# Two token tiles through each stage transition of a two-block network: together, or one ahead of the other

## What is computed

```
x = [256, 1024]                                   # BATCH 1, SEQ 256
for i in range(2):                                # first block
    sh1, sc1, g1, sh2, sc2, g2 = split(silu(c) @ ada_w[i] + ada_b[i])
    h = rms_norm(x, norm_mix[i]) * (1 + sc1) + sh1
    y = chunked_relpos_attention(h) if i == 0 else chunked_spatial_gating(h)
    x = x + g1 * y
    h = rms_norm(x, norm_ffn[i]) * (1 + sc2) + sh2
    x = x + g2 * (square(relu(h @ ffn_w1[i])) @ ffn_w2[i])
for l in range(2):                                # second block
    h = rms_norm(x, pre_norm_g[l]);  proj = h @ w_in[l]      # q, k, v, gates of two attentions
    y = concat(ya, yb) @ w_out[l]
    x = x + rms_norm(y, post_norm_g[l])
```

## Time and profile before

| | us |
|---|---|
| median of 3 runs | 1133.7 (1127.31 to 1136.37) |
| the profiled execution's own time | 1133.17 |
| its span, first to last instruction | 1131.5 |
| PE busy | 1081.2 |
| DVE busy | 768.0 |
| ACT busy | 554.4 |
| mean granted TensorE clock | 0.947 of full |

### The profile page before, as it was taken

The page is one execution under the profiler, slowest core; times in us unless marked ns, Lnnn a source line. Parts: engine busy times, 40 slices in busy tenths (PEclk is TensorE's granted clock), DMA queues, the critical chain, the costliest instruction groups (busy, mean ns, idle before and its releaser), DMA issues.

```text
span 1131.5 us, 18346 instructions
## 1 busy us (share of the span) xinstructions
PE 1081.2 (96%) x6096; PEld 931.3 (82%) x6096; DVE 768.0 (68%) x1352; ACT 554.4 (49%) x933; POOL 92.4 (8%) x146
## 2 busy tenths in 40 slices
PE   6998979999999999999999999999999989899897
PEld 6877867899989878889998789998878768688685
DVE  5787667887887567777877555465487464675663
ACT  1556756434543356634443344354355563545552
POOL 1121101000000000100000000000011020120100
PEclk8799988799999889999999799999999999799989
DMA  9875555588778358865765265546266410466111
GB/s 373 314 256 193 196 187 186 171 295 292 268 268 298 135 179 280 302 216 201 254 220 189 88 212 201 177 164 216 67 211 221 137 56 20 158 206 202 57 33 51
DMA packets 58071, 219.12 MB, mean 194 GB/s; under 512 B 6532, under 2 KB 12420, under 8 KB 51880
## 3 DMA queue, kind: packets, MB, share of 16 engines
q1 hardware_dynamic: 49232, 170.02, 43.7%
q0 software_dynamic: 5760, 41.95, 10.4%
q10 hardware_dynamic: 3032, 6.57, 1.8%
HBM read 217.46 MB, written 1.06 MB: 193 GB/s over the span
## 4 chain that ended last, share of the span: by engine, by line
PE 78%; issue 8%; DVE 7%; DMA 2%; ACT 2%; POOL 2%; DVEq 0%; SPq 0%; ACTq 0%; POOLq 0%
PE ps L1593 23%; PE ps L1594 22%; PE ps L1595 22%; PE ps L1660 2%; PE ps L1688 2%; DVE w_lo L947 2%; PE ps L1678 1%; PE ps L1642 1%; POOL rinv L439 1%; DMA ada_raw<-in_adastream 1%; PE ps L1955 1%; PE ps L1652 1%; ACT ada_raw L630 1%; PE ps L2061 1%; DVE h_lo L1028 1%
## 5 line engine op out<-in xcount | busy, mean ns | idle before, releaser
L947 DVE TENSOR_TENSOR w_lo<-raw,w_hi 128x1024 fp32r<-128x1024 f32 (+1 forms) x318 | 359.3, 1172 | 58.9 <-ACT w_hi L533 53.2
L533 ACT ACTIVATE w_hi<-raw 128x1024 fp32r<-128x1024 f32 (+1 forms) x318 | 308.7, 1009 | 127.9 <-DMA raw<-in_wstream 90.7
L1593 PE MATMUL ps<-h_hi,w_hi 128*128 128x256 f32 x704 | 203.1, 288 | 0.7 <-DVE h_lo L1028 0.5
L1595 PE MATMUL ps<-h_hi,w_lo 128*128 128x256 f32 x704 | 201.4, 286 | 0.0
L1594 PE MATMUL ps<-h_lo,w_hi 128*128 128x256 f32 x704 | 201.4, 286 | 0.0
L1593 PE MATMUL ps<-w_hi,h_hi 128*128 128x512 f32 (+1 forms) x480 | 193.8, 404 | 3.2 <-DVE h_lo L1028 3.2
L1594 PE MATMUL ps<-w_lo,h_hi 128*128 128x512 f32 (+1 forms) x480 | 188.3, 392 | 0.0
L1595 PE MATMUL ps<-w_hi,h_lo 128*128 128x512 f32 (+1 forms) x480 | 188.2, 392 | 0.0
L1593 PEld LDWEIGHTS ps<-h_hi,w_hi 128*128 128x128 f32 x704 | 137.6, 195 | 3.7 <-issue 2.2
L1593 PE MATMUL ps<-w_hi,a_hi 128*128 128x512 f32 x352 | 137.4, 390 | 0.7 <-DVE a_lo L1356 0.7
L1594 PEld LDWEIGHTS ps<-h_lo,w_hi 128*128 128x128 f32 x704 | 137.4, 195 | 0.7
(11 more groups left out here) (186 smaller groups left out, 1347.7 us busy)
## 6 DMA issues: line engine op xcount, KB each, us to landing
raw<-in_wstream SPq DMA_DIRECT2D x296, 512.0 KB, 5.4
ada_raw<-in_adastream POOLq DMA_DIRECT2D x40, 1024.0 KB, 5.4
ada_raw<-in_adastream SPq DMA_DIRECT2D x4, 1024.0 KB, 9.0
arena<-in_adastream SPq DMA_DIRECT2D x4, 1024.0 KB, 10.6
raw<-in_wsmall SPq DMA_DIRECT2D x22, 128.0 KB, 2.2
row<-in_gate_rows ACTq DMA_DIRECT2D x5, 512.0 KB, 3.9
row<-in_params ACTq DMA_DIRECT2D x2, 769.0 KB, 4.0
x<-in_x SPq DMA_DIRECT2D x1, 1024.0 KB, 9.0
```

The costliest lines, as they stand in the source:

```text
L533: act.activation(w_hi[:, c % SPLIT, at], raw[:, n, 0:width // 2], ACT.Copy)\
L947: nc.vector.tensor_tensor(w_lo[:, c % SPLIT, at], raw[:, (2 * c + h) % RAW, 0:width // 2], w_hi[:, c % SPLIT, at].bitcast(F32), ALU.subtract)\
L1593: nc.tensor.matmul(dst, sh, mh, start=start, stop=False)
L1595: return nc.tensor.matmul(dst, sl, mh, start=False, stop=stop)
```

## The change

**Every transition runs tile by tile.** The last products of a stage are ordered so that tile 0's banks end first (`last_downs`: tile 0's products of both chunks, then tile 1's; the attention's and the second block's output steps likewise). The residual, the squares, the scaling, the transposes, the modulation and the operand's split are then written for one tile at a time, in halves of four k-blocks: 128-column ACT instructions in place of 256-column ones (twice as many), the same number of transposes and of DVE instructions. PE issues 4 matmuls of zeros before tile 0's transposes and 8 behind them. The first products of the next stage are made for tile 0, then tile 1 is transposed between them, then tile 1's products follow.

**In the FFNs** the first two `up` chunks are therefore made with the tokens stationary (`up_tile`, 96 matmuls of 256 columns, as many as before); their results are copied out by ACT, transposed back by PE (`turn_up`, 4 transposes for each chunk) and then go through relu and square.

**In the gating** the shift and scale columns (`columns(36, 4)`) move between tile 0's and tile 1's last products, and DVE's last two conditioning sums (`ada(46)`, `ada(47)`) move from before the transition to behind it. In the attention `columns(12, 5)` moves ahead of tile 1's last two output steps.

**In the second block** the four small chunks become one chunk of full width (`heads_tile`), `project_tile` runs over two chunks (CL+1, CL+2) with the second tile's transposes between them, the layers and the gating's groups are written out instead of looped, and the splits next to the transitions are placed anew: of chunk CL+2, `lo_part(CL + 2, 0)` comes behind tile 0's operand and `lo_part(CL + 2, 1)` behind tile 1's.

Shortened to what the text below speaks of (ACT's part first, then DVE's, then PE's):

```diff
+            def square(t, count):
+
+                act.wait_ge(s_res, count)
+                act.activation(both[:, t * D:(t + 1) * D], x[:, t, :], ACT.Square,
+                               accum_out=ss2[:, t:t + 1]).then_inc(s_sq, 1)
+
+            def modulate(t, count, scale, shift):
+
+                for half in range(2):
+                    act.wait_ge(s_xT, count + 2 * t + half + 1)
+                    for k in range(4 * half, 4 * half + 4):
+                        last = act.activation(f[:, k, t * P:(t + 1) * P],
+                                              ps[:, 4 + 2 * t + half, (k % 4) * P:(k % 4 + 1) * P],
+                                              ACT.Identity, scale=scale[:, k:k + 1],
+                                              bias=shift[:, k:k + 1] if shift is not None
+                                              else zero_col[:])
+                    last.then_inc(s_f, 1)
...
+
+                split(c0 + 3)
+                for u in range(2):
+                    act.wait_ge(s_used, c0 + u + 1)
+                    act.activation(squared[:, u, :], ps[:, 2 * u, :], ACT.Copy)\
+                        .then_inc(s_upraw, 1)
+                    act.wait_ge(s_upT, m0 // 14 + u + 1)
+                    act.activation(relu[:, u, :], ps[:, 4 + u, :], ACT.Relu).then_inc(s_upread, 1)
+                    act.wait_ge(s_upread, 2 + m0 + u + 1)
+                    act.activation(a_hi[:, u].rearrange("p a b -> p (a b)"), relu[:, u, :],
+                                   ACT.Square).then_inc(s_acthi, 1)
+                for j in range(1, 4):
+                    split(c0 + 3 + j)
...
+            split(C_WO + 5)
+            square(0, 1)
...
+            modulate(0, 4, mod_scale[:, 1], mod_shift[:, 1])
+            square(1, 2)
+            modulate(1, 4, mod_scale[:, 1], mod_shift[:, 1])
+            split(C_WO + 6)
...
-                squares(4, lambda t: act.wait_ge(s_res, layer * 2 + (6 + t + 1)))
-
...
+
+                act.wait_ge(s_pre, layer * 16 + 16)
+                modulate(0, layer * 4 + 16, prenorm, None)
...
-                    act.wait_ge(s_xT, layer * 4 + (16 + pr + 1))
-                    for b in range(2):
-                        k = 2 * pr + b
-                        last = act.activation(f[:, k, :], ps[:, 4 + pr, b * S:(b + 1) * S],
-                                              ACT.Identity, scale=prenorm[:, k:k + 1],
...
+
+                i = 2 * t + cb
+                dve.wait_ge(*ready[i])
+                cut = slice(cb * 512, (cb + 1) * 512)
+                own.inc(nc.vector.tensor_tensor(y_tmp[:, i, :], ps[:, cb * 2 + t, :], gate[:, cut],
+                                                ALU.mult))
+                own.wait()
+                last = nc.vector.tensor_tensor(x[:, t, cut], x[:, t, cut], y_tmp[:, i, :], ALU.add)
+                if cb == 1:
+                    last.then_inc(s_res, 1)
...
+            def transition(ready, count, at_first, before_second, behind):
+
+
+                residual(0, 0, ready)
+                residual(0, 1, ready)
+                at_first()
+                residual(1, 0, ready)
+                norm_x(0, count // 2)
+                residual(1, 1, ready)
+                operand(0, count)
+                before_second()
+                norm_x(1, count // 2)
+                operand(1, count)
+                behind()
...
+                modulation(1, 5)
+                lo_part(C_WO + 4, 1, CW)
...
-                    operand(8)
+                    transition(ready, 8, lambda: None, lambda: lo_part(c0 + 34, 0, CW),
+                               lambda: lo_part(c0 + 34, 1, CW))
                 else:
...
+            def gated_modulation():
+                modulation(3, 4)
+
+            transition([(s_bank, 4), (s_bank, 5), (s_bank, 6), (s_used, C_FFN[1])], 12,
+                       gated_modulation, lambda: None, lambda: split(C_FFN[1] + 2))
+            ada(46)
+            ada(47)
             mlp_stage(1, 28, False)
...
+                norm_x(0, layer * 2 + 8)
+                operand(0, layer * 4 + 16)
+                lo_part(CL + 2, 0, CW)
+                norm_x(1, layer * 2 + 8)
+                operand(1, layer * 4 + 16)
+                lo_part(CL + 2, 1, CW)
+                lsplit(3)
...
+                if layer + 1 < DEPTH:
+                    lsplit(C_LAYER)
...
+                if layer + 1 < DEPTH:
+                    lsplit(C_LAYER + 1)
...
+            def project_tile(c, bank, h_base, t, between=None):
+
+                for half in range(2):
+                    chunk_in(c + half)
+                    for n in range(4):
+                        k = half * 4 + n
+                        operand_in(h_base, t, k)
+                        last = matmul3(ps[:, bank, :], tokens(k, t), weights(c + half, 512, n),
+                                       k == 0, k == KT - 1)
                     if t == 1:
                         last.then_inc(s_used, 1)
-
...
+                for k in range(KT):
+                    last = nc.tensor.transpose(
+                        ps[:, 4 + 2 * t + k // 4, (k % 4) * P:(k % 4 + 1) * P],
+                        xn[:, t, k * P:(k + 1) * P], ident[:])
+                    if k % 4 == 3:
+                        last.then_inc(s_xT, 1)
+
+            def transition(count):
+                keep_warm(7, WARM[0])
+                transpose_x(0, count)
+                keep_warm(7, WARM[1])
...
+            def up_tile(c, u, t, ks, h_base):
+
+                for k in ks:
+                    operand_in(h_base, t, k)
+                    last = matmul3(ps[:, 2 * u, t * AW:(t + 1) * AW], tokens(k, t),
+                                   weights(c + u, AW, k), k == 0, k == KT - 1)
+                if t == 1 and ks[-1] == KT - 1:
+                    last.then_inc(s_used, 1)
+
+            def turn_up(u, count):
+
+                pe.wait_ge(s_upraw, count + u + 1)
+                for b in range(2):
+                    for t in range(TT):
+                        last = nc.tensor.transpose(
+                            ps[:, 4 + u, b * S + t * P:b * S + (t + 1) * P],
+                            squared[:, u, t * AW + b * P:t * AW + (b + 1) * P], ident[:])
+                last.then_inc(s_upT, 1)
...
+                for t in range(TT):
+                    for u in range(2):
+                        if t == 0:
+                            chunk_in(c + 2 + u)
+                            pe.wait_ge(s_act, m + u + 1)
+                        for cb in range(2):
+                            last = down_products(c, u, t, cb, u == 1)
+                            if u == 1 and (t, cb) != (1, 1):
+                                last.then_inc(s_bank, 1)
+                        if t == 1:
+                            last.then_inc(s_used, 1)
+                    if t == 0 and between is not None:
+                        between()
...
+                transition(2 * n)
+                chunk_in(c0)
+                up_tile(c0, 0, 0, range(KT), 4 * n + 4)
+                transpose_x(1, 2 * n)
+                chunk_in(c0 + 1)
+                up_tile(c0, 1, 0, range(KT), 4 * n + 4)
+                up_tile(c0, 0, 1, range(KT), 4 * n + 4)
+                up_tile(c0, 1, 1, range(4), 4 * n + 4)
+                turn_up(0, 2 * layer)
+                up_tile(c0, 1, 1, range(4, KT), 4 * n + 4)
+                for bank in (0, 1, 3):
+                    zero_bank(bank)
+                turn_up(1, 2 * layer)
+                zero_bank(2)
+                for u in range(2):
+                    down(c0, u, m0 + u, None, 4, lambda v: v)
+                with pe.Fori(0, 6) as i:
                     for u in range(2):
-                        up(c0, u, m0 + u, i, 4, lambda v: i * 2 + v, h_base)
...
+            transition(4)
+            pe.wait_ge(s_gelu, 2)
+            project_tile(C_GV, 0, 12, 0, lambda: transpose_x(1, 4))
+            project_tile(C_GV, 1, 12, 1)
...
+            def gated_columns():
+                pe.wait_ge(s_upread, 2 + 28)
+                pe.wait_ge(s_ada, 44)
+                columns(36, 4)
...
+                else:
+                    last_downs(c, m, gated_columns)
...
+                def heads_tile(t):
+                    chunk_in(CL)
+                    for k in range(KT):
+                        operand_in(layer * 8 + 20, t, k)
+                        last = matmul3(ps[:, t, 0:S], tokens(k, t), weights(CL, S, k), k == 0,
+                                       k == KT - 1)
+                    last.then_inc((s_half, s_used)[t], 1)
...
+                heads_tile(0)
+                project_tile(CL + 1, 2, layer * 8 + 20, 0,
+                             lambda: transpose_x(1, layer * 2 + 8))
+                heads_tile(1)
+                project_tile(CL + 1, 3, layer * 8 + 20, 1)
```

More of the change, by code:

```diff
@@ L486, in _ @@
             norm(3)
-            with pool.Fori(0, DEPTH) as layer, own.loop(layer, DEPTH, 15):
+            for layer in range(DEPTH):
```

(11 more changed lines are left out.)

558 lines of the change are left out of this document (258 added, 300 removed).

## The result

| | before | after |
|---|---|---|
| median, us (15 runs each) | 1133.35 (1127.31 to 1139.92) | 1142.53 (1138.1 to 1147.15) |
| profiled execution's own time, us | 1133.17 | 1139.18 |
| its span, us | 1131.5 | 1137.5 |
| mean granted clock | 0.947 | 0.953 |

The ratio is 1.0082, 95% interval 1.0058 to 1.0107: some 9.2 us slower by the medians, where 10.6 had been predicted.

The account below looks back on a forecast made before the run. PE's own time was taken as the bound (busy 96%), with losses in five transition gaps and half clock behind them. Terms -0.8 - 3.2 + 0.4 + 5.6 + 8.2 + 0.4 = +10.6 on 1133.17 gave 1143.8 us; range 1126 to 1153.

Parts of the forecast that it names:

- rival A: The forecast itself: second-tile waits and half clock as summed, 1134 to 1153 us; chance 0.6.
- second-tile waits: PE waiting inside stages for work queued behind tile 1's operand: 4.9 us in each second-block layer's `project_tile`.
- transition 2: FFN 0 to gating: first product at E+4.2 (E is the last product's end), gap and block -3.2 us.
- Transition 4: FFN 1 to layer 0: first product E+5.6, 4.9 us wait in `project_tile`, half clock 2.5; +5.6 us in all.
- transition 5: Layer 0 to layer 1: first product E+12.1 or E+13.3, the same 4.9 us wait and half clock; +8.2 us.
- Transition 1: Attention to FFN 0: first product at 199.8 (before 203.7), down products at 216.5 against 217.9; -0.8 us.
- the wait of 1.4 for the conditioning sum: Transition 1: PE reaches the moved columns at 183.6 and waits 1.4 us for DVE's sum, ending near 185.1.
- the 1.7 us before tile 1's transposes at transition 2: Transition 2: PE has made half of tile 0's products by E+7.0 and waits 1.7 us for tile 1's norm.
- Transition 3: Gating to FFN 1: earlier first product, but two conditioning sums delay the first activation, PE idle some 3.6 us; +0.4 us.
- B: Rival: the clock stays up behind the gaps; -2.8 us, 1130 us (1125 to 1136); chance 0.2.
- C: Rival: the second tile's work is never late, leaving gaps and transposes alone; -22 us, 1111 us (to 1122); chance 0.08.
- D: Rival: chunk CL+4 comes late, each second-block layer losing 5 us more; 1154 us (1148 to 1160); chance 0.12.

Follow-up runs that it names:

- experiment 1: Changed kernel with both halves of chunk CL+2 split ahead of tile 1's norm and modulation in both second-block layers; 1133.89 us, ratio 1.0022 to the kernel before.
- experiment 2: Changed kernel with the gating's last two conditioning sums moved back ahead of the transition to FFN 1; 1136.17 us, ratio 1.0029 to the kernel before.
- experiment 4: Changed kernel with the edits of experiment 1 and experiment 2 together; 1127.59 us, ratio 0.9957 to the kernel before.
- experiment 5: Experiment 4 with DVE's norm of tile 0 ahead of tile 1's last residual, and between layers ahead of chunk CL+1's split; 1122.32 us, ratio 0.9894.
- experiment 6: Experiment 4 without the zero matmuls at the transitions (0 and 0 instead of 4 and 8); 1126.68 us, ratio 0.9946 to the kernel before.
- number 9: All edits of experiment 4, experiment 5, experiment 6 and experiment 8 joined on the changed kernel; 1116.55 us, ratio 0.9834 to the kernel before.
- Experiment 8: Experiment 4 with both tiles squared, normed and transposed before the first product in the second block only; 1118.99 us, ratio 0.9862 to the kernel before.

## Why the prediction came out as it did

**Right, by its own steps.** The forecast was rival A's: second-tile waits and half clock behind them, +10.6. The waits were found where they were placed and at their size: 4.9 predicted, 4.89 and 4.89 measured on `w_lo` in the middle of `project_tile`; 3.6 predicted, 3.54 measured on `a_lo` in FFN 1. So was ACT's new form: eight 128-column instructions at 2.9, taken between the bounds 2.1 and 3.75, took 2.91. First products: E+4.2 against 4.6 at transition 2, E+5.6 against 6.5 at 4, E+12.1 to 13.3 against 13.1 at 5; 199.8 against 199.38 at 1, where the wait of 1.4 for the conditioning sum measured 1.27. What made this work is that each wait was summed along three lists (PE's transposes, ACT's eight, DVE's operand and low part) and not taken from shares. Experiments 1, 2 and 4 show the waits, with the half clock behind them, to be the cause: without them the sign turns. One wait did not appear: the 1.7 us before tile 1's transposes at transition 2. Half clock stretched the products ahead of it from 2.7 to 4.4 us and filled it whole, so it added nothing; in experiment 5, where the clock stayed up there, PE waited 1.04.

**Mis-sized terms.** Transition 4 was +8.1 for +5.6. The term that was too small is the half clock: I took it once, 2.5 us. The trace has it on both sides of the wait, some 1.7 us in the first products (821.34 to 825.3) and 2.1 behind the wait, and the eight zeros behind the transposes, priced at nothing, took 3.26 us, part of them at half clock, and ended 0.8 after the operand was ready. Between the layers, where that had been allowed for, they ended 1.5 after it. Transition 1 came out at -1.8 for both its parts against -0.8, transition 2 at -4.2 against -3.2. Transition 3 was +2.8 against +0.4: the first down product was due up to 2.9 us sooner than before and came no sooner (0.0), and for the half clock behind its wait the sum leaves about 1.2 us, where it took 2.5. These errors have both signs, and the total of the transitions, +12.6, is two above the forecast. That the median came within 1.3 us of 1143.8 is in part luck.

**Rivals.** B (the clock stays up, 1130) fell: all five blocks stand at 0.78 to 0.91 and the gap of 4.5 us at transition 2 is followed by 0.88. (Its own sum has a slip: with the 4.9 of waiting transition 5 comes to 12.1 + 22.5 - 31.6 = +3.0 and not +4.7.) The Trainium skill, TensorE: Matmul & The Clock Gate, section "HAM oscillation — how this bites in real kernels", asks for short idle gaps to keep PE warm. This case agrees only in part. In the gap at transition 2 PE was idle for just 0.61 us, the rest being zeros and transposes, and half clock came all the same, a microsecond into the products; in experiments 1, 5 and 6 the same place stayed at 1.00. And where the prediction has the trace agree that long gaps are followed by half clock, it passes over the longest, 18.2 us, which was followed by 1.00. So behind these gaps half clock is partly a matter of the execution. C (second tile never late) fell with the waits; but its 1111 to 1122 was within reach: number 9 has 1116.55, with items moved in the lists, no zeros, and the tile-by-tile start given up in the second block. D (chunk CL+4 late) did not happen: beside the two waits of 4.9, no wait for `w_lo` of note is left in the group's 11.2 us.

**What I did not see.** The prediction took the tile-by-tile order at transitions 4 and 5 as a gain that waits spoil. Numbers 6 and 8 show that there is no gain there: with one tile or with both, the first product comes 6.1 and 11.7 us behind E, so bringing tile 1 along costs it nothing.

## What to carry to other kernels

When a stage is cut so that one half's work starts early, list for each engine what stands between the half's operand and everything that the running half still needs; a weight part queued behind the second half's operand turns an early start into a wait. Moving such items was worth 14 us here, more than the change itself cost: half a chunk's split one place ahead in two lists, and two conditioning sums ahead of the transition in DVE's. Price a wait in the middle of products at more than its length, since the products behind it ran at half clock (2.1 and 2.5 us more here). And before splitting, ask whether the second half is ready in time anyway; in the second block it was, and starting both together won.

## What the runs showed of the hardware

- One-row zeros did not keep the clock up (0.82 and 0.79 with them, 0.87 and 0.79 without); with 128-row identity matmuls it stayed at 1.00 through a gap of 18.7 us. The Trainium skill, TensorE: Matmul & The Clock Gate, section "Part 4: PE-mode transpose", says that transposes do not count as activity for the clock in the way matmuls do. Experiment 8 differs: between the layers PE was idle for 6.58 us, then ran sixteen transposes and nothing else (0.50 from 968.9 to 972.0), and the products behind them ran at 1.00 (972.9 to 989.6).
- An ordinary float32 matmul of 128 columns is two instructions of 0.11 us in the trace (x132 for 66, 14.90 us), an f32 transpose of the same size one (x8 for 8, 1.04 us).
- The same 32 one-column matmuls were followed by half clock in one execution and by 1.00 in the other; of the clock a single profile says little.
